# Sampled attention in a two-group decoder layer: the value products with the cached values as stationary operand

## What is computed

```python
def slc_attend(q, qpos, kb, vb, idx):          # selected blocks, idx per token and kv head
    kg = kb[bi, hi, idx]
    vg = vb[bi, hi, idx]
    s = jnp.einsum('bqhgd,bhqnsd->bhgqns', q, kg).astype(jnp.float32) * SCALE
    p, _ = masked_softmax(s, mask, (-2, -1))
    return jnp.einsum('bhgqns,bhqnsd->bqhgd', p.astype(vg.dtype), vg)

def window_attend(q, k_all, v_all, qpos):      # the last 512 keys
    s = jnp.einsum('bnqhgd,bnkhd->bnhgqk', qq, kg).astype(jnp.float32) * SCALE
    p, _ = masked_softmax(s, mask[None, :, None, None], (-1,))
    o = jnp.einsum('bnhgqk,bnkhd->bnqhgd', p.astype(vg.dtype), vg)

def dilated_group(q, k_all, v_all, w, d):      # (w, d) = (128, 1), (512, 4), (2048, 16), 2 heads each
    s = jnp.einsum('bqhd,bqkhd->bhqk', qb, kg).astype(jnp.float32) * SCALE
    p, lse = masked_softmax(s, valid[None, None], (-1,))
    o = jnp.einsum('bhqk,bqkhd->bqhd', p.astype(vg.dtype), vg)
```

## Time and profile before

| | |
|---|---|
| time, median of 3 runs | 1973.58 us (1971.96 to 1975.07) |
| profiled execution, first to last instruction | 1964.2 us |
| mean clock granted to TensorE in it | 0.876 |
| TensorE busy, matmuls | 1856.2 us, 95% |
| TensorE loads of stationary operands | 1657.3 us, 84% |
| VectorE, ScalarE, GpSimd busy | 739.1, 592.4, 98.9 us |
| share of the chain that ended last | PE 84%, DMA 6%, DVE 4% |
| sampled attention's value products (L1112) in that chain | 7% |

### The profile page before, as it was taken

How to read it: one execution, slowest core, us unless ns; L and a number is a source line. 1 busy time by engine, 2 the same in 40 slices (tenths; PEclk the granted TensorE clock), 3 DMA queues, 4 the chain that set the end, 5 groups by cost and what they waited for, 6 DMA issues and landing times.

```text
span 1964.2 us, 30472 instructions
## 1 busy us (share of the span) xinstructions
PE 1856.2 (95%) x12307; PEld 1657.3 (84%) x12307; DVE 739.1 (38%) x1475; ACT 592.4 (30%) x1122; POOL 98.9 (5%) x118
## 2 busy tenths in 40 slices
PE   5999999988999998999899999999998899999998
PEld 4888888988999998999655667777667799999998
DVE  3333336322423346354465761111015633223332
ACT  2444443221223322323332452221112333212221
POOL 0000000000000000000400002121100000000000
PEclk9999999988999999999655895555557999999999
DMA  8232230334646331122230006455421222323331
GB/s 291 106 152 85 91 123 1 120 130 172 207 151 218 93 106 55 61 86 80 77 86 1 1 20 166 144 150 146 114 74 43 65 86 85 104 71 92 87 104 60
DMA packets 183079, 201.68 MB, mean 103 GB/s; under 512 B 9847, under 2 KB 167006, under 8 KB 180382
## 3 DMA queue, kind: packets, MB, share of 16 engines
q1 hardware_dynamic: 167109, 111.10, 18.7%
q0 software_dynamic: 11536, 89.10, 13.4%
q10 hardware_dynamic: 4352, 0.34, 0.2%
HBM read 195.29 MB, written 31.40 MB: 115 GB/s over the span
## 4 chain that ended last, share of the span: by engine, by line
PE 84%; DMA 6%; DVE 4%; issue 1%; SPq 1%; ACT 1%; POOL 1%; ACTq 0%; DVEq 0%; POOLq 0%; PEldq 0%
PE PS L773 16%; PE PS L775 16%; PE PS L774 16%; PE PS L724 11%; PE PS L1112 7%; PE PS L1040 3%; PE PS L1005 3%; PE PS L712 3%; DMA WR<-in_ffn_in 2%; PE PS L1019 2%; PE PS L1086 2%; DMA BIG<-in_cache_slc_kv,IXS 1%; DMA BIG<-in_cache_dil_kv 1%; SPq L552 1%; DVE QTR L1581 1%
## 5 line engine op out<-in xcount | busy, mean ns | idle before, releaser
L773 PE MATMUL PS<-HNH,WHI 128*128 128x272 f32 x1408 | 411.1, 292 | 26.6 <-DVE WLO L1503 16.0
L774 PE MATMUL PS<-HNL,WHI 128*128 128x272 f32 x1408 | 408.6, 290 | 0.0
L775 PE MATMUL PS<-HNH,WLO 128*128 128x272 f32 x1408 | 407.8, 290 | 0.0
L773 PEld LDWEIGHTS PS<-HNH,WHI 128*128 128x128 f32 x1408 | 268.7, 191 | 30.6 <-issue 27.2
L1192 ACT ACTIVATE WHI<-WR 128x1024 fp32r<-128x1024 f32 (+3 forms) x144 | 164.4, 1151 | 348.9 <-DMA WR<-in_ffn_in 165.2
L775 PEld LDWEIGHTS PS<-HNH,WLO 128*128 128x128 f32 x1408 | 269.2, 191 | 0.0
L774 PEld LDWEIGHTS PS<-HNL,WHI 128*128 128x128 f32 x1408 | 269.1, 191 | 0.0
L1503 DVE TENSOR_TENSOR WLO<-WR,WHI 128x1024 fp32r<-128x1024 f32 (+3 forms) x144 | 192.3, 1343 | 195.0 <-ACT WHI L1192 194.0
L773 PE MATMUL PS<-HIDH,WHI 128*128 128x272 f32 x704 | 202.5, 288 | 0.0
L775 PE MATMUL PS<-HIDH,WLO 128*128 128x272 f32 x704 | 202.5, 288 | 0.0
L774 PE MATMUL PS<-HIDL,WHI 128*128 128x272 f32 x704 | 202.1, 287 | 0.0
(11 more groups left out here) (304 smaller groups left out, 2663.9 us busy)
## 6 DMA issues: line engine op xcount, KB each, us to landing
WR<-in_ffn_in SPq DMA_DIRECT2D x88, 512.0 KB, 3.7
WR<-in_ffn_out SPq DMA_DIRECT2D x32, 704.0 KB, 4.4
out_dil_s<-in_cache_dil_kv POOLq DMA_DIRECT2D x8, 2044.0 KB, 9.2
WR<-in_w_in SPq DMA_DIRECT2D x14, 648.0 KB, 4.8
BIG<-in_cache_dil_kv SPq DMA_DIRECT2D x8, 512.0 KB, 6.7
WR<-in_cache_dil_kv SPq DMA_DIRECT2D x8, 512.0 KB, 5.6
WR<-in_w_out SPq DMA_DIRECT2D x8, 512.0 KB, 3.8
out_win_s<-in_cache_win_kv POOLq DMA_DIRECT2D x2, 2032.0 KB, 22.2
```

The source lines that it names most:

```text
L773: pe.matmul(out, a[0], b[0], start=first, stop=False)
L774: pe.matmul(out, a[0], b[1], start=False, stop=False)
L775: return pe.matmul(out, a[1], b[0], start=False, stop=last)
```

## The change

The value products change their operands' parts: the tile of cached values (both kv heads, 128 columns) is loaded, and the exponentials stream: 3 columns (the heads of one kv head) for a selected tile, 24 for the window, 8 for a dilated group. The result has the head dimension on its partitions and the query rows along the columns, so `rows_out` and `turned` go, with their semaphores; the sum of the denominators moves to the end of `values(b)`, ahead of `pv`, and waits for `sums` there. PSUM banks 6 and 7 hold the results of even and odd sequences, so `values(b)` waits for `outs(b - 2)` and no longer for `rows_out(b - 1)`, and `outs` reads PSUM behind `pv`.

The new keys and new values are padded to whole tiles: `newK` gives the 128 columns of four neighbouring items, `newV` all 128 rows of `VV[:, 4]`, set to zero at the start. `SMX` becomes a tensor of 128 columns of its own and `SDG` one of 128 rows, so `top` and `spread` are 128 by 128 too. `top(b)` waits for the subtraction of b - 1 instead of `outs`. `sums(b)` waits for `values(b - 1)`, since `SSUM` is read later. In the diff a line with three dots marks left out lines.

```diff
--- before.py
+++ after.py
@@ -204,11 +204,12 @@
-        QN = sb("QN", [P, 11, NS])
+        QN = sb("QN", [P, 14, NS])
...
-        SDG = sb("SDG", [56, 57])
+        SMX = sb("SMX", [P, P])
+        SDG = sb("SDG", [P, 57])
@@ -253,7 +254,7 @@
-                                          "rev", "ot", "out", "ex")}
+                                          "out", "ex")}
@@ -356,11 +357,10 @@
-        ODR, OSR, OWR = VVf[0:8, 1008:1392], VVf[0:6, 1392:1904], VVf[0:24, 1904:2032]
...
-        SMX, SSUM, SINV, SWG = (SA[:, n, :] for n in range(4))
+        SSUM, SINV, SWG = (SA[:, n, :] for n in range(3))
@@ -376,8 +376,8 @@
-        newK = lambda item: QN[:, item, :]
-        newV = lambda c: VV[0:NS, 4, c:c + P]
+        newK = lambda item: QN[:, item:item + 4, :].rearrange("p i n -> p (i n)")
+        newV = lambda c: VV[:, 4, c:c + P]
@@ -400,22 +400,18 @@
         def value_tiles(b):
...
-            w, kv, ex = b % 2, KV[b % 3], EXS[b % 2]
+            w, kv, ex, out = b % 2, KV[b % 3], EXS[b % 2], PS[:, 6 + b % 2, :]
...
-                    cols = lambda j: (2 * t + h) * 1024 + j * 256 + P + h * HD
-                    tiles = [(of_token(ex[0:SEL7, 24 * j:24 * j + 24], t), kv[0:SEL7, cols(j):cols(j) + HD])
-                             for j in range(4)]
-                    tiles.append((of_token(ex[0:NS, 96:120], t), VV[0:NS, 4, h * HD:(h + 1) * HD]))
-                    yield PS[0:6, 6, t * P + h * HD:t * P + (h + 1) * HD], tiles
-            at = lambda t, j: t[:, j * 256 + P:(j + 1) * 256]
-            yield PS[0:24, 7, 0:P], [(ex[:, 120 + 24 * j:144 + 24 * j], at(KWIN[w], j)) for j in range(4)] \
-                + [(ex[0:NS, 216:240], newV(P))]
-            yield PS[0:8, 7, P:2 * P], [(ex[:, 240:248], at(KDL0[w], 0)), (ex[0:NS, 312:320], newV(256))]
-            yield PS[0:8, 7, 2 * P:3 * P], [(ex[:, 248 + 8 * j:256 + 8 * j], at(KDL1[w], j)) for j in range(4)] \
-                + [(ex[0:NS, 320:328], newV(256 + P))]
-            yield PS[0:8, 7, 3 * P:4 * P], [(ex[:, 280 + 8 * j:288 + 8 * j], at(KDL2[w], j)) for j in range(4)] \
-                + [(ex[0:NS, 328:336], newV(256 + 2 * P))]
+                    own = lambda c: of_token(ex[:, c:c + 24], t)[:, 3 * h:3 * h + 3]
+                    cols = lambda j: (2 * t + h) * 1024 + j * 256 + P
+                    tiles = [(kv[0:SEL7, cols(j):cols(j) + P], own(24 * j)[0:SEL7]) for j in range(4)]
+                    yield of_token(out[:, 0:24], t)[:, 3 * h:3 * h + 3], tiles + [(newV(0), own(96))]
+            for at, R, V_, n, c, new in ((24, 24, KWIN, 4, 120, P), (48, 8, KDL0, 1, 240, 256), (56, 8, KDL1, 4, 248, 256 + P),
+                                         (64, 8, KDL2, 4, 280, 256 + 2 * P)):
+                tiles = [(V_[w][:, j * 256 + P:(j + 1) * 256], ex[:, c + R * j:c + R * (j + 1)]) for j in range(n)]
+                fresh = 216 if R == 24 else 312 + at - 48
+                yield out[:, at:at + R], tiles + [(newV(new), ex[:, fresh:fresh + R])]
@@ -1076,7 +1072,7 @@
                     if x == NGR:
...
-                        ps = PS[0:NS, 2 + b % 2, :]
+                        ps = PS[:, 2 + b % 2, :]
@@ -1094,47 +1090,34 @@
                 pe.wait_ge(sa["mx"], b + 1)
...
-                    pe.wait_ge(sa["out"], b)
-                pe.transpose(PS[0:56, 5, 0:P], SMX, ident).then_inc(sa["mt"], 1)
+                    pe.wait_ge(sa["sub"], b)
+                pe.transpose(PS[:, 5, 0:P], SMX[:, :], ident).then_inc(sa["mt"], 1)
...
             def spread(b):
...
-                pe.matmul(PS[:, 5, P:P + 56], ones[0:56, :], SDG[:, 1:57], start=True, stop=True).then_inc(sa["bc"], 1)
+                pe.matmul(PS[:, 5, P:P + 56], ones, SDG[:, 1:57], start=True, stop=True).then_inc(sa["bc"], 1)
...
             def values(b):
...
-                if b:
-                    pe.wait_ge(sa["rev"], 3 * b)
+                if b >= 2:
+                    pe.wait_ge(sa["out"], b - 1)
...
-                    for y, (ex, v) in enumerate(tiles):
-                        mm = pe.matmul(dst, ex, v, start=(y == 0), stop=(y == len(tiles) - 1))
-                mm.then_inc(sa["pv"], 1)
-
-            def turned(b):
-
-                pe.wait_ge(sa["rev"], 3 * b + 3)
-                for t in range(TS):
-                    pe.transpose(of_token(PS[:, 5, 192:216], t), OSR[:, t * P:(t + 1) * P], ident[0:6, 0:6])
-                pe.transpose(PS[:, 5, 216:240], OWR, ident[0:24, 0:24])
-                for g in range(3):
-                    pe.transpose(PS[:, 5, 240 + 8 * g:248 + 8 * g], ODR[:, g * P:(g + 1) * P], ident[0:8, 0:8])
+                    for y, (v, ex) in enumerate(tiles):
+                        pe.matmul(dst, v, ex, start=(y == 0), stop=(y == len(tiles) - 1))
...
-                pe.matmul(PS[:, 5, 264:320], ones, SSUM, start=True, stop=True).then_inc(sa["ot"], 1)
+                pe.matmul(PS[:, 6 + b % 2, 72:128], ones, SSUM, start=True, stop=True).then_inc(sa["pv"], 1)
...
             for b in range(NB):
                 for x in range(NGR + 1):
...
-                    if x == 1 and b:
-                        turned(b - 1)
...
-            turned(NB - 1)
@@ -1411,28 +1394,17 @@
-            def rows_out(b):
-                act.wait_ge(sa["pv"], b + 1)
-                if b:
-                    act.wait_ge(sa["ot"], b)
-                act.activation(OSR, PS[0:6, 6, :], ACT.Copy).then_inc(sa["rev"], 1)
-                act.activation(OWR, PS[0:24, 7, 0:P], ACT.Copy).then_inc(sa["rev"], 1)
-                act.activation(ODR, PS[0:8, 7, P:4 * P], ACT.Copy).then_inc(sa["rev"], 1)
-
             act.wait_ge(pa["pv"], 3 * NU)
...
             for x in range(NGR):
...
             for b in range(NB):
                 for x in range(NGR):
-                    if x == 1 and b:
-                        rows_out(b - 1)
...
-            rows_out(NB - 1)
@@ -1471,6 +1443,8 @@
             dve.wait_ge(ix_mm, 1)
...
+            V.memset(VV[:, 4, :], 0.0)
+            V.memset(QN[:, 11:14, :], 0.0)
@@ -1898,6 +1872,7 @@
             dve.wait_ge(pa["oev"], NU)
+            V.memset(SMX[:, :], 0.0)
@@ -1924,12 +1899,12 @@
             def maxima(b):
...
-                over_tiles(SCO, SMX, ALU.max).then_inc(sa["mx"], 1)
+                over_tiles(SCO, SMX[:, 0:56], ALU.max).then_inc(sa["mx"], 1)
...
             def diagonal(b):
...
-                link(V.tensor_reduce(SDG[:, 0:1], PS[0:56, 5, 0:P], AX.X, ALU.max))
-                V.tensor_scalar(SDG[:, 1:57], ident[0:56, 0:56], SDG[:, 0:1], None, ALU.mult).then_inc(sa["dg"], 1)
+                link(V.tensor_reduce(SDG[:, 0:1], PS[:, 5, 0:P], AX.X, ALU.max))
+                V.tensor_scalar(SDG[:, 1:57], ident[:, 0:56], SDG[:, 0:1], None, ALU.mult).then_inc(sa["dg"], 1)
@@ -1946,11 +1921,13 @@
             def sums(b):
...
+                if b:
+                    dve.wait_ge(sa["pv"], b)
...
             def outs(b):
-                dve.wait_ge(sa["ot"], b + 1)
-                ps = PS[:, 5, 192:320]
+                dve.wait_ge(sa["pv"], b + 1)
+                ps = PS[:, 6 + b % 2, 0:128]
```

## The result

| | before | after |
|---|---|---|
| median of the runs, us | 1972.77 (1970.91 to 1975.07, 4 runs) | 2027.25 (2002.31 to 2029.15, 4 runs) |
| the profiled execution's span, us | 1964.2 | 2025.0 |
| TensorE's mean granted clock in it | 0.876 | 0.861 |
| eight values blocks (with the sum over ones after), us | 144.2 | 198.0 |

The forecast was 2031 us, range 2018 to 2042.

The account below looks back on a forecast made before the run. The prediction took the sampled attention as bound by TensorE and a transfer starting only when a values block ends. Terms 53.5 + 10.3 - 0.3 - 0.4 - 5.3 = +57.8 us on 1973.6 gave 2031 us, range 2018 to 2042.

Parts of the forecast that it names:

- The price: TensorE products loading 128 columns: 0.213 us each at half clock, the load being paid whether 3, 8 or 24 columns stream.
- (a): Values blocks: 116 instructions at 0.213 us make 24.7 us instead of 18.0; +53.5 us over eight sequences, all on the chain.
- (b): Padded new keys: ten 128-column loads cost +1.5 us each time, on the chain for seven sequences; +10.3 us.
- (c): Maxima's transposition and `spread`, padded: one more load width, one row-count change less; -0.3 us, counted once.
- (d): `rows_out` and `turned` removed from the gaps: the transfer is late next, so only -0.4 us is kept.
- (e): Gaps after values blocks: the 3.4 us of full clock go, but the transfer covers the loss.
- (f): After the last two blocks, nothing covers `rows_out` and `turned`; removing them and an earlier `top` give together -5.3 us.
- (g): Added memsets at the start and ahead of the first keys: run on an idle vector engine, 0 us.
- W: Rival: products on the whole array wake the clock to full, values blocks take 13.0 us; 1926 us, chance 0.05.
- L: Rival: cheaper 128-column loads in values blocks; 1936 us at 0.11 each (chance 0.03), 2008 us in between (0.04).
- S: Rival: each new accumulation group in a values block empties the array, 0.2 us each; 2050 us, chance 0.04.
- N: Rival: in values blocks, saved waits offset longer loads at 0.16 us per instruction, so no change; 1974 us, chance 0.01.

Follow-up runs that it names:

- e9: Changed kernel loading only one kv head's 64 columns for selected tiles, both heads in the same half of the array, second head's results missing: 1962.93 us.
- e2: Changed kernel loading only the kv head's own 64 columns for selected tiles, results to that head's 64 partitions: 1939.18 us, ratio 0.9817.
- e4: Changed kernel with the new keys on 32 columns again, all else changed: 2015.31 us, ratio 1.0282.
- e7: The kernel before, run and profiled once more without any change: 1969.61 us, ratio 0.9993.
- e5: Changed kernel with 112 columns streaming in every value product, surplus results overwritten or unread: 1956.14 us, ratio 0.9917.
- e3: Kernel before with only the new values' tiles and their exponentials padded to 128 rows, operands otherwise as before: 1910.92 us, ratio 0.9681.
- e6: Changed kernel with the page gathers of the second and third sequence held back until the first one's key steps are nearly done: 2028.21 us, ratio 1.0353.

## Why the prediction was right, point by point

**The price** (0.213 per instruction with 128 columns loaded): right, 24.32 / 114 = 0.213, with 3, 8 and 24 streaming columns, no "issue" waits, a clock of 0.50. e9 and e2 show that it goes by the columns loaded. The Trainium skill (TensorE: Matmul & The Clock Gate, "LDWEIGHTS (loading the stationary operand)") has the proportion to columns right, but its 0.107 us for 128 columns is half of the 0.213 that an instruction of these fp32 products takes here at half clock.

**(a) the values blocks**, +53.5: measured +53.8.

**(b) the padded new keys**, +10.3, seven of 1.5: measured 13.5 (six gaps 10.9 by e4, the start 2.6), so the term was a quarter too small: the 1.5 us of added work in a gap are as put, and 0.3 us of waits in each came on top. The new keys of a sequence stand ahead of the values of the one before it: those of the first two sequences lie in the stage's start, and nothing covered them there, since TensorE was late there itself; in the last gap there are none. The product rows after read 0.42 us from one pair to the next, the 0.213 each that I took:

```profile
1486.56 0.60 PE L1076 MATMUL PS<-QA,QN 128*128 128x24 f32 x2
1486.99 0.60 PE L1077 MATMUL PS<-QA,QN 128*128 128x24 f32 x2
1487.41 1.43 PE L1079 MATMUL PS<-QD,QN 128*128 128x8 f32 x6
```

**(c), (d) and (e) the gaps**, -0.7 in all: too little. e4's six gaps without the padded keys sum to 114.2 us against 119.6 of before, -5.4, 0.9 each (-7.6 against the 121.8 of e7). I had let the transfer eat what `rows_out` and `turned` free, on the ground of one gap in which it had landed 0.9 us before TensorE came; in e4 TensorE is busy 18.50 of 18.50 us in the window over the first gap's bulk, 1243.2 to 1261.7: it, not the transfer, was last there. Over the six gaps TensorE is busy for 110.8 us in e4 and for 111.4 before: at the colder clock its work takes as long without `turned` as it did with it. What fell is its waits, from 8.2 us to 3.5. That the lost 3.4 us of full clock cost nothing on balance holds: all gaps are at 0.50 and are still 20.2 to 21.4 us long, where I said 21 to 22. The two errors, (b) 3.2 too small and this 4.7 too small a gain, cancel but for 1.5. That was luck, and makes the sum look surer than these two terms were.

**(f) the last gap and the end**, -3.1 and -2.2: measured -3.4 and -2.1. The timeline behind the seventh block and behind the last, which answer to the earlier trace rows:

```profile
1514.72 0.65 PE L1110 MATMUL PS<-SA,CO 128*128 128x56 f32 x2
...
1515.41 0.51 DVE L1931 RECIPROCAL SA<-PS 128x56 f32<-128x56 f32 x1 [23.11 <-PE PS L1110]
...
1518.95 1.87 PE L1108 MATMUL PS<-VV,BIG 112*128 112x3 f32 x8 [1.24 <-ACT VV L1405]
...
1543.29 0.65 PE L1110 MATMUL PS<-SA,CO 128*128 128x56 f32 x2
...
1543.98 0.51 DVE L1931 RECIPROCAL SA<-PS 128x56 f32<-128x56 f32 x1 [24.13 <-PE PS L1110]
```

The weights come 0.5 us after the block instead of 2.3, as put.

**(g) the memsets**, 0: no wait on them shows in the chain.

**The rivals.** W is refuted in time and mechanism (24.6 us of uninterrupted work on the whole array at 0.50, e5). L is refuted: 0.213 in all of a block, with 112 rows or 128 and with 3, 8 or 24 columns streaming, at half clock. S: no stop at any of the 12 groups, 24.3 us for seven blocks and 24.5 for the last. N would need 0.16 per instruction. The Trainium skill says under "The HAM clock gate" of the same page that sustained activity releases the clock. In these blocks the measurement says otherwise: TensorE is busy for 24.60 of 24.60 us and the clock stays at 0.50.

**The start of the count.** The profiled execution of before spans 1964.2 us. I put the 9.4 us to the median down to what lies outside the span; in all results of the study a run's time is 1.8 us over its span, so it was mostly one execution without the standstill. That did no harm, since the sum was set on the median. The listed chances add up to 0.91 for slower and 0.08 for faster, where it says 0.90 and 0.09; nothing hangs on that.

**Open.** Single runs of both kernels lie some 25 us below the others (2002.31 with a mean clock of 0.873 here, against 0.859 to 0.861; 1941.55 with 0.892 among the runs of e7, against 0.871 to 0.881). None of them was profiled, so where their clock is higher, and why, is not known.

## What to carry to other kernels

When products are bound by the load of the stationary operand, load the operand with few columns and stream the other, or put narrow loads into the two halves of the columns in turn (e2). A short tile among full ones costs more than itself: padding its rows with zeros (e3, one memset and a few slices) brought 3.2% here, by the half-clock prices 18 us from the stops that go and 40 from the clock that comes up. Padding the side that is loaded brings nothing and costs its columns (e4).

## What the runs showed of the hardware that I had not expected

- The clock stayed at 0.50 from 1171 to 1556 us in the changed kernel with TensorE busy for 358.4 of 385 us, and rose inside the values blocks of e3 and e5 with the engine no busier. Both stream 64 to 128 columns per instruction without a stop between; the kernel before streams as many as e3, with a stop of 0.2 to 0.4 us after every ten instructions, and stays at 0.50 for 10 us.
- Loads of 64 columns in alternating halves of the array, at half clock: 0.067 us each, against 0.107 in one half (e2, e9).
- ScalarE waited 5 and 9 us for something that the profile does not name, and TensorE with it, while sixteen gathers of pages kept the DMA engines at a share of 1.02; in both kernels (e7). With the gathers held back the same copies did not wait, and the standstill came again beside the later gathers (e6); in one profile a share of 1.03 went without it.
